# Norm weights and sub-keys of a two-layer decoder kept on chip for both chunks of a layer

## Chip, core and metric

The kernel runs on one core of one Trainium2 chip, all in float32, batch 1, 256 positions of width 1024. The metric is the device time of one execution in microseconds; the median of several executions counts.

## What is computed

Two decoder layers. Layer 0 mixes tokens with a state-space model (S5), layer 1 with dilated window attention; after each mixer stands PEER, a channel mixer that picks 16 of 16384 single-neuron experts for each of 8 heads and each token. Every sub-layer has an RMS norm with its own weight vector ahead of it, and a last norm ends the program. Cut to what matters:

```python
for i in range(2):
    h = rms_norm(x, norm_mix[i])
    x = x + (s5_mixer(h, ...) if i == 0 else dilated_attention_mixer(h, ...))
    h = rms_norm(x, norm_ffn[i])
    x = x + peer_ffn(h, peer_w_q[i], peer_sub_keys[i], peer_u[i], peer_v[i])
return rms_norm(x, norm_final)

def rms_norm(x, g):
    return x * rsqrt(mean(x * x) + 1e-6) * g

def peer_ffn(h, w_q, sub_keys, u_tab, v_tab):
    q = (h @ w_q).reshape(bsz, seq, 8, 2, 128)
    s = einsum('blhpe,hpne->blhpn', q, sub_keys)      # 16 tables of 128 keys
    ...                                               # top 16 of each half, top 16 of the sums
    act = einsum('cd,ckd->ck', hc, u_tab[ic])         # 128 experts per token
    return einsum('ck,ckd->cd', gc * gelu(act), v_tab[ic])
```

Five norm weight vectors are used: `norm_mix[0]`, `norm_ffn[0]`, `norm_mix[1]`, `norm_ffn[1]`, `norm_final`. They are rows 0 to 4 of the array `gains`.

## The kernel before

The 256 positions are two chunks of 128, one position per partition. The work of a chunk in a layer is: norm, mixer, norm, PEER scores and top-16, then the gathers of the experts. There are four gather phases (phase = 2 x layer + chunk) of 128 gathers each, 512 in all. A gather (L1233, issued by GpSimd) fetches one expert row of 8 KB (its u and its v vector) for each of the 128 partitions, 1 MB in all, into one of the eight slots of `ringmem`. Gathers come in pairs: VectorE multiplies u with the token and sums it into `dots` (L1262), ScalarE makes the gated weight (L820, L825, tile `S`), TensorE adds v (L448) and so frees the slots (semaphore `v_pe`); GpSimd issues gather s only when gather s-8 has been freed.

A chunk's gathers run beside the layer work of the next one: phase 0 beside the S5 mixer of chunk 1, phase 1 beside the attention of chunk 0, phase 2 beside the attention of chunk 1, phase 3 alone. The interleaving is written out by hand: each engine's program calls `g.at(phase, n)`, which puts the pairs up to number n ahead of the next piece of layer work. The constants at L345 to L357 (`S5_AT`, `QKV_AT`, `WO_AT` and others) set the places.

All plain loads are issued by SyncE (SP) in one fixed order, each after the waits that stand ahead of it. A weight item is 2 MB (`wt`, two buffers used in turn; item n waits for `w_used >= n-1`, the projection of item n-2). In layer 1 a chunk's items are 18 of `w_qkv`, two of `w_o`, four of `w_q`.

- One buffer `gain` (1024 floats per partition) holds the norm weight in use. `next_gain(e, n)` (L391 to L393) waits until norm number e-1 is done (`normed >= e`) and then loads row n for all partitions, 512 KB. There are nine such loads.
- The 16 key tables (`keysT`, 8 KB per partition, 1 MB) are a view into `area`, a work space that the mixers also use. So they are loaded for every phase, by `load_keys` (L395 to L397), once the mixer has left that part of `area`: behind `glu_done` in layer 0, behind `o_turned` (the transposes of the attention output, L772) in layer 1. There are four such loads. In layer 1 this load stands between the first and the second item of `w_o`, so the second item is not issued before `o_turned`.
- The users: VectorE's norm (L1287 to L1291 and L1306 to L1310) waits for `gain_in`; TensorE's score products wait for `keys_in`.

GpSimd writes the descriptors of its gathers into a part of the on-chip memory that is set aside for them, 16 KB of each partition where the program names no size.

Of the kernel before, what the change touches and what calls it, by code (L numbers as in the profile page):

```python
# [94 lines left out]
def build(nc, x, gains, lam, b_in, c_out, d_skip, w_glu, w_qkv, w_o, w_q, keys, experts, consts,  # L95
          masks, out):
    ctx = ExitStack()
    with ctx:
# [9 lines left out]
        Hrep = sb("Hrep", [P, QUAD, D])  # L108
        hT = sb("hT", [P, KT, P])
        gT = sb("gT", [P, KT, P])  # L110
        gain = sb("gain", [P, D])
        wt = sb("wt", [P, 2, KT, BLOCK])
        ringmem = sb("ringmem", [P, RING * 2 * D])
        area = sb("area", [P, A_WORDS])
# [61 lines left out]

        gflat = gT[:, :, :].rearrange("p k t -> p (k t)")
        keysT = view(area, 12288, HP, NKEYS)
        qT = view(area, 14336, 2, QHP, P)  # L180
        qs = sb("qs", [P, 512])

# [51 lines left out]
        skip_in = sem("skip_in")  # L234
        zeroed = sem("zeroed")
        wb_in = sem("wb_in")
        gain_in = sem("gain_in")
        keys_in = sem("keys_in")
        mask_in = sem("mask_in")
        w_in = [sem(f"w_in{k}") for k in range(2)]  # L240
# [119 lines left out]

        @block.sync
        def _(sp):
            sp.dma_start(small[:, 0:3, :], lam).then_inc(lam_in, 16)
            sp.dma_start(con[:, 0:C_IOTA], consts[:, 0:C_IOTA]).then_inc(ramp_in, 16)
            sp.dma_start(X[:, 0, :], x[0:P, :]).then_inc(x_in[0], 16)
            sp.dma_start(gain[:, :], gains[0:1, :].to_broadcast([P, D])).then_inc(gain_in, 16)
            sp.dma_start(WB.rearrange("p a b c -> p (a b c)"), b_in).then_inc(wb_in, 16)
            sp.dma_start(craw[:, :, :, :], c_out).then_inc(craw_in, 16)
            sp.dma_start(con[:, C_IOTA:C_ALL], consts[:, C_IOTA:C_ALL]).then_inc(con_in, 16)
            sp.dma_start(skip[:, :], d_skip).then_inc(skip_in, 16)  # L370
            sp.dma_start(X[:, 1, :], x[P:2 * P, :]).then_inc(x_in[1], 16)

            def weights(layer, c, first, last):

                for i in range(first, last):
                    n = item(layer, c, i)
                    if layer == 0:
                        src = w_glu[i] if i < WQ0 else w_q[0, i - WQ0]
                    elif i < WO:
                        src = w_qkv[i]  # L380
                    elif i < WQ1:
                        src = w_o[i - WO]
                    else:
                        src = w_q[1, i - WQ1]
                    if n == 1:
                        sp.wait_ge(glu_used, 2)
                    if n >= 2:
                        sp.wait_ge(w_used, n - 1)
                    sp.dma_start(wt[:, n % 2].rearrange("p k n -> p (k n)"), src).then_inc(w_in[n % 2], 16)

            def next_gain(e, n):  # L391
                sp.wait_ge(normed, e)
                sp.dma_start(gain[:, :], gains[n:n + 1, :].to_broadcast([P, D])).then_inc(gain_in, 16)  # L393

            def load_keys(phase, ready, count):  # L395
                sp.wait_ge(ready, count)
                sp.dma_start(keysT, keys[phase // NC]).then_inc(keys_in, 16)  # L397

            for i in range(4):
                sp.dma_start(wglu[i].rearrange("p k n -> p (k n)"), w_glu[i]).then_inc(glu_in[i], 16)  # L400
            weights(0, 0, 4, 5)
            next_gain(1, 1)
            weights(0, 0, 5, 6)
            load_keys(0, glu_done, 1)
            next_gain(2, 0)
            sp.wait_ge(glu_used, 4)
            for i in range(2):
                sp.dma_start(wq_ring[i].rearrange("p k n -> p (k n)"), w_q[0, 2 + i]).then_inc(wq_in[i], 16)
            weights(0, 1, 0, 1)
            next_gain(3, 1)  # L410
            sp.wait_ge(idx_ready, event(0, QUARTERS - 1))
            weights(0, 1, 1, 6)
            load_keys(1, glu_done, 2)
            weights(0, 1, 6, 8)
            for c in range(NC):
                next_gain(4 + 2 * c, 2)
                weights(1, c, 0, 2)
                next_gain(5 + 2 * c, 3)
                weights(1, c, 2, 8)
                sp.wait_ge(score_done, event(1 + c, QUARTERS - 1))  # L420
                n = NG * P * (c + 1)
                sp.dma_start(mask[:, 0:n], masks[:, M_AT[c]:M_AT[c] + n]).then_inc(mask_in, 16)
                weights(1, c, 8, WO + 1)
                load_keys(2 + c, o_turned, c + 1)
                weights(1, c, WO + 1, ITEMS1)
            next_gain(8, 4)
            for c in range(NC):
                sp.wait_ge(out_ready, c + 1)
                sp.dma_start(out[c * P:(c + 1) * P, :], H[:, :]).then_inc(out_done, 16)
            sp.wait_ge(out_done, 16 * NC)  # L430
# [3 lines left out]
        def _(pe):  # L434
# [93 lines left out]
            def peer_scores(gphase, layer, c, at_norm, at_wq):  # L528
# [3 lines left out]
                for i in range(QUARTERS + 1):  # L532
                    g.at(gphase, at_wq + i)
                    if i == 0:
                        pe.wait_ge(hT_ready, e + 1)
                    if i < 2:
                        spread_next(ph, (2 * i, 2 * i + 1))
                    if i < QUARTERS:
                        project_turned(item(layer, c, (WQ0, WQ1)[layer] + i), 4 + i)
                    if i == 1:  # L540
                        pe.wait_ge(keys_in, 16 * (ph + 1))
                    if i >= 1:
                        pe.wait_ge(q_copied, event(ph, i - 1))
                        for m in range(QHP):
                            hp = QHP * (i - 1) + m
                            last = pe.matmul(ps[:, 3 + i, m * P:(m + 1) * P], qT[:, (i - 1) % 2, m, :],  # L546
                                             keysT[:, hp, :], start=True, stop=True,
                                             skip_group_check=True)
                        last.then_inc(score_done, 1)
# [690 lines left out]
        def _(v):  # L1240
# [42 lines left out]
                                ALU.add).then_inc(var_ready, 1)  # L1283

            def norm_scale(c, e, done, h_free, count):
                v.wait_ge(root_ready, e + 1)
                link(v.reciprocal(stat[:, 3:4], stat[:, 2:3]))  # L1287
                v.wait_ge(gain_in, 16 * (min(e, 8) + 1))
                if count:
                    v.wait_ge(h_free, count)  # L1290
                v.scalar_tensor_tensor(out=H[:, :], in0=X[:, c, :], scalar=stat[:, 3:4],  # L1291
                                       in1=gain[:, :], op0=ALU.mult, op1=ALU.mult).then_inc(done, 1)

            def norm(gphase, start, c, e, done, h_free, count):
                norm_sum(c)
# [3 lines left out]
            def norm_halves(c, e):  # L1299
# [4 lines left out]
                                ALU.add).then_inc(var_ready, 1)  # L1304
                v.wait_ge(root_ready, e + 1)
                link(v.reciprocal(stat[:, 3:4], stat[:, 2:3]))  # L1306
                v.wait_ge(gain_in, 16 * (e + 1))
                for half in range(2):
                    cols = slice(half * 512, (half + 1) * 512)
                    v.scalar_tensor_tensor(out=H[:, cols], in0=X[:, c, cols], scalar=stat[:, 3:4],  # L1310
                                           in1=gain[:, cols], op0=ALU.mult,
                                           op1=ALU.mult).then_inc((h_half, normed)[half], 1)

            def s5_lambda():
# [447 lines left out]
```

## Time and profile before

| | us |
|---|---|
| median of 3 runs | 1752.63 (1750.5 to 1753.52) |
| span of the profiled execution | 1755.3 |

| engine | busy, us | share of the span |
|---|---|---|
| TensorE, matmul | 1285.1 | 73% |
| TensorE, weight load (beside the matmuls) | 544.9 | 31% |
| VectorE | 1120.6 | 64% |
| ScalarE | 677.5 | 39% |
| GpSimd | 616.7 | 35% |

The core's DMA engines moved 685.81 MB. The profile gives the profiled execution's span, from the first to the last instruction, and no separate time around it. In the tables of stages a DMA share of 1.0 says that all 16 DMA engines had a packet under way throughout; the rate in GB/s beside it says what they moved. "PEclk" is the granted TensorE clock as a share of full speed. In a timeline the bracket behind a row is the time in which the engine sat idle before it, with what ended it.

### The profile page before, as it was taken

Reading aid. Unit: us, or ns where it says so; the run is one execution under the profiler, and the core shown is the slowest. Engines: PE = TensorE matmul, PEld = TensorE weight load, DVE = VectorE, ACT = ScalarE, POOL = GpSimd, SP = SyncE. Lnnn points to the kernel's source line nnn. Section 1 sums busy time; section 2 is a strip of 40 time slices with the busy share of each in tenths; the row PEclk is TensorE's granted clock in tenths of the full one; section 3 lists DMA queues with packets and bytes.
Section 4 is the critical chain, followed back from the end, with each engine's and each line's share of the span. In section 5 each row is a group of like instructions: output and inputs, shape, how many; then the busy total and the mean of one; then the engine's idle time right before and its main releaser. Section 6 shows DMA issues by size and latency. Waiting matters only on the chain.

```text
span 1755.3 us, 17565 instructions
## 1 busy us (share of the span) xinstructions
PE 1285.1 (73%) x5714; PEld 544.9 (31%) x5714; DVE 1120.6 (64%) x2526; ACT 677.5 (39%) x2033; POOL 616.7 (35%) x557
## 2 busy tenths in 40 slices
PE   3876565666969968997788895899886975545454
PEld 2463111222713313333244331543451810000000
DVE  8967999863568765436347966553554567676544
ACT  7643232322243257128134333821652233233222
POOL 4213444442242243224223323332442144444442
PEclk9988877688989979998899998999997976786878
DMA  8099999999999999999999999999999899999997
GB/s 332 7 367 378 380 366 390 392 407 422 424 420 423 424 422 421 426 422 421 423 414 418 415 423 411 381 386 424 422 379 423 332 333 411 418 418 412 420 421 299
DMA packets 86636, 685.81 MB, mean 391 GB/s; under 512 B 9872, under 2 KB 10256, under 8 KB 12176
## 3 DMA queue, kind: packets, MB, share of 16 engines
q0 software_dynamic: 73728, 536.90, 74.9%
q1 hardware_dynamic: 12816, 147.79, 20.3%
q8 instruction: 45, 0.74, 0.2%
q14 instruction: 47, 0.39, 0.1%
HBM read 683.60 MB, written 1.05 MB: 390 GB/s over the span
## 4 chain that ended last, share of the span: by engine, by line
PE 34%; DMA 33%; DVE 19%; ACT 6%; issue 5%; POOL 2%; SPq 0%; POOLq 0%; ACTq 0%; DVEq 0%
DMA ringmem<-experts,lay 24%; PE ps L509 11%; PE ps L448 11%; PE ps L523 6%; DMA wt<-w_qkv 6%; DVE ringmem L1262 6%; POOL ringmem L1233 2%; DMA wt<-w_o 2%; ACT S L825 1%; ACT lay L898 1%; PE ps L727 1%; PE ps L702 1%; PE ps L461 1%; PE ps L713 1%; DMA wt<-w_glu 1%
## 5 line engine op out<-in xcount | busy, mean ns | idle before, releaser
L1233 POOL DMA_INDIRECT ringmem<-experts,lay x512 | 585.3, 1143 | 1062.4 <-PE ps L448 932.0
L448 PE MATMUL ps<-ringmem,S 128*32 128x512 f32 x2048 | 618.2, 753 | 368.3 <-ACT S L825 364.3
L1262 DVE CUSTOM_DVE_ANT_0 ringmem<-ringmem,Hrep 128x1024 f32<-128x1024 f32 x384 | 461.1, 1224 | 260.4 <-DMA ringmem<-experts,lay 257.9
L448 PEld LDWEIGHTS ps<-ringmem,S 128*32 128x32 f32 x2048 | 112.6, 126 | 761.7 <-ACT S L825 516.4
L820 ACT ACTIVATE gelus<-dots 128x2 f32<-128x2 f32 x256 | 51.5, 201 | 628.7 <-DVE dots L1262 624.0
L509 PE MATMUL ps<-wt,hT 128*128 128x512 f32 x576 | 256.2, 598 | 13.8 <-DMA wt<-w_qkv 13.8
L1262 DVE CUSTOM_DVE_ANT_0 ringmem<-ringmem,area 128x1024 f32<-128x1024 f32 x128 | 155.6, 1225 | 110.6 <-DMA ringmem<-experts,lay 110.0
L509 PEld LDWEIGHTS ps<-wt,hT 128*128 128x128 f32 x576 | 106.7, 190 | 164.1 <-issue 153.8
L816 ACT ACTIVATE S<-con,lay 128x32 f32<-128x32 f32 x512 | 134.6, 311 | 39.7 <-PE ps L448 39.1
L825 ACT ACTIVATE S<-S,gelus 128x32 f32<-128x32 f32 x512 | 136.8, 314 | 24.6 <-ACT gelus L820 1.1
L523 PEld LDWEIGHTS ps<-hT,wt 128*128 128x128 f32 x896 | 104.4, 197 | 12.1 <-issue 11.9
L523 PE MATMUL ps<-hT,wt 128*128 128x128 f32 x896 | 107.3, 282 | 0.0
L509 PE MATMUL ps<-wt,gT 128*128 128x512 f32 x128 | 63.2, 652 | 12.6 <-DMA wt<-w_o 10.5
L820 ACT ACT_TABLE_LOAD x55 | 70.6, 1283 | 1.0
L898 ACT COPY lay<-sel 32x16 f32<-32x16 f32 (+1 forms) x272 | 54.4, 200 | 18.8 <-DVE sel L1586 15.8
L1090 ACT COPY area<-ps 128x512 f32<-128x512 f32 x12 | 7.0, 586 | 135.3 <-PE ps L509 135.3
L1607 DVE TENSOR_TENSOR area<-ps,con 128x512 f32<-128x512 f32 x24 | 16.6, 690 | 65.9 <-PE ps L509 56.7
L1622 DVE CUSTOM_DVE_ANT_0 area<-ps,area 128x384 f32<-128x384 f32 (+1 forms) x32 | 24.2, 757 | 46.2 <-PE ps L702 46.2
L1510 DVE MAX8 qs<-ps 128x8 f32<-128x128 f32 x56 | 12.6, 285 | 62.0 <-PE ps L546 47.4
L1262 DVE DVE_READ_ACCUMULATOR2_ANT dots<- 128x1 f32 x512 | 42.1, 82 | 0.0
L509 PEld LDWEIGHTS ps<-wt,gT 128*128 128x128 f32 x128 | 26.1, 209 | 50.8 <-issue 34.6
L1065 ACT ACT_TABLE_LOAD x32 | 41.1, 1283 | 0.6
(234 smaller groups left out, 1237.1 us busy)
## 6 DMA issues: line engine op xcount, KB each, us to landing
wt<-w_qkv SPq DMA_DIRECT2D x36, 2048.0 KB, 11.6
wt<-w_q SPq DMA_DIRECT2D x14, 2048.0 KB, 11.3
wt<-w_glu SPq DMA_DIRECT2D x5, 2048.0 KB, 11.9
ringmem<-experts,lay POOLq DMA_INDIRECT x512, 12.5
wt<-w_o SPq DMA_DIRECT2D x4, 2048.0 KB, 14.4
ringmem<-w_glu SPq DMA_DIRECT2D x3, 2048.0 KB, 21.5
gain<-gains SPq DMA_DIRECT2D x9, 512.0 KB, 11.1
area<-keys SPq DMA_DIRECT2D x4, 1024.0 KB, 9.6
```

The costliest lines, as they stand in the source:

```text
L448: last = pe.matmul(ps[TG * t:TG * (t + 1), half, :], S[:, u % 2, i, :], ring[:, (2 * u + i) % RING, D + half * 512:D + (half + 1) * 512], ...
L461: pe.matmul(ps[:, bank, :], rep[rows_j, :], H[rows_j, half * 512:(half + 1) * 512], start=True, stop=True, skip_group_check=True).then_inc ...
L509: last = pe.matmul(ps[:, bank, :], act[:, k, :], wt[:, n % 2, k, :], start=(k == 0), stop=(k == KT - 1))
L523: last = pe.matmul(ps[:, bank, m * P:(m + 1) * P], w[:, k, m * P:(m + 1) * P], hT[:, k, :], start=(k == 0 and m == parts[0]), stop=(k == K ...
L816: last = act.activation(S[:, u % 2, i, :], own, ACT.Copy, scale=lay[:, phase % NC, 1, j - 1 + i, n:n + 1])
L820: act.activation(gelus[:, u % 2, :], dots[:, u % 2, :], ACT.Gelu_apprx_tanh).then_inc(gelu_ready, 1)
L825: last = act.activation(S[:, u % 2, i, :], S[:, u % 2, i, :], ACT.Copy, scale=gelus[:, u % 2, i:i + 1])
L898: last = act.copy(lay[TG * r:TG * (r + 1), ph % NC, :, j, n:n + width], sel[TG * j:TG * (j + 1), :, at + width * r:at + width * (r + 1)])
L1065: act.activation(SS[u % 2][:, 0:n], SS[u % 2][:, 0:n], ACT.Exp, bias=nmx[:, u:u + 1], scale=DH ** -0.5, accum_out=den[:, u:u + 1]).then_in ...
L1233: pool.indirect_dma_start(ring[:, s % RING, :], None, experts[phase // NC], bass.IndirectOffsetOnAxis(ap=rows[:, phase % NC, j, n:n + 1], ...
L1262: last = v.tensor_tensor_reduce(ring[:, i, 0:D], ring[:, i, 0:D], hrep(phase, j), 1.0, 0.0, ALU.mult, ALU.add, dots[:, b, second:second + 1])
L1622: v.tensor_tensor_reduce(SS[u % 2][:, 0:n], banks(2, 4)[:, at:at + n], mask[:, 0:n], 1.0, NEG, ALU.add, ALU.max, mx[:, u:u + 1]).then_inc( ...
```

## The change

The norm weights get two buffers, one for the norms ahead of the mixers (rows 0, 2 and 4 of `gains`) and one for the norms ahead of PEER (rows 1 and 3), and the keys get a buffer of their own outside `area`. Each weight vector is loaded once and each layer's keys once, for both chunks. That is 4 KB and 8 KB per partition more; the room for gather descriptors is cut from 16 KB to 4 KB per partition. The waits and places of the loads in SP's order change with it.

```diff
-        gain = sb("gain", [P, D])
+        gains_at = [sb("gain_mix", [P, D]), sb("gain_ffn", [P, D])]
+        keysT = sb("keysT", [P, HP, NKEYS])
...
-        keysT = view(area, 12288, HP, NKEYS)
...
-        gain_in = sem("gain_in")
+        gain_in = [sem("gain_mix_in"), sem("gain_ffn_in")]
...
+            def load_gain(n):
+                which = n % 2
+                sp.dma_start(gains_at[which][:, :],
+                             gains[n:n + 1, :].to_broadcast([P, D])).then_inc(gain_in[which], 16)
+
+            def load_keys(layer):
+                sp.dma_start(keysT[:, :, :], keys[layer]).then_inc(keys_in, 16)
...
             def next_gain(e, n):
-                sp.wait_ge(normed, e)
-                sp.dma_start(gain[:, :], gains[n:n + 1, :].to_broadcast([P, D])).then_inc(gain_in, 16)
-
-            def load_keys(phase, ready, count):
-                sp.wait_ge(ready, count)
-                sp.dma_start(keysT, keys[phase // NC]).then_inc(keys_in, 16)
+                sp.wait_ge(normed, e + 1)
+                load_gain(n)
...
             weights(0, 0, 4, 5)
-            next_gain(1, 1)
+            load_gain(1)
+            load_keys(0)
             weights(0, 0, 5, 6)
-            load_keys(0, glu_done, 1)
-            next_gain(2, 0)
             sp.wait_ge(glu_used, 4)
             for i in range(2):
                 sp.dma_start(wq_ring[i].rearrange("p k n -> p (k n)"), w_q[0, 2 + i]).then_inc(wq_in[i], 16)
             weights(0, 1, 0, 1)
-            next_gain(3, 1)
+            next_gain(norm_event(0, 1, 0), 2)
             sp.wait_ge(idx_ready, event(0, QUARTERS - 1))
-            weights(0, 1, 1, 6)
-            load_keys(1, glu_done, 2)
-            weights(0, 1, 6, 8)
+            weights(0, 1, 1, 8)
+            next_gain(norm_event(0, 1, 1), 3)
             for c in range(NC):
-                next_gain(4 + 2 * c, 2)
-                weights(1, c, 0, 2)
-                next_gain(5 + 2 * c, 3)
-                weights(1, c, 2, 8)
+                weights(1, c, 0, 8)
                 sp.wait_ge(score_done, event(1 + c, QUARTERS - 1))
+                if c == 0:
+                    load_keys(1)
                 n = NG * P * (c + 1)
                 sp.dma_start(mask[:, 0:n], masks[:, M_AT[c]:M_AT[c] + n]).then_inc(mask_in, 16)
-                weights(1, c, 8, WO + 1)
-                load_keys(2 + c, o_turned, c + 1)
-                weights(1, c, WO + 1, ITEMS1)
-            next_gain(8, 4)
+                weights(1, c, 8, ITEMS1)
+            next_gain(norm_event(1, 1, 0), 4)
...
-                        pe.wait_ge(keys_in, 16 * (ph + 1))
+                        pe.wait_ge(keys_in, 16 * (layer + 1))
...
-                v.wait_ge(gain_in, 16 * (min(e, 8) + 1))
+                v.wait_ge(gain_in[which], 16 * (min(e, 8) // 4 + 1))
...
-    nc = bacc.Bacc("TRN2", target_bir_lowering=False, num_devices=1)
+    nc = bacc.Bacc("TRN2", target_bir_lowering=False, num_devices=1, dynamic_dma_scratch_size=4096)
```

## Rows read from the trace of the kernel before

**Rows 1.** The page, what the DMA engines moved in 40 slices of 43.9 us

```profile
GB/s 332 7 367 378 380 366 390 392 407 422 424 420 423 424 422 421 426 422 421 423 414 418 415 423 411 381 386 424 422 379 423 332 333 411 418 418 412 420 421 299
```

**Rows 2.** Table of stages: start:end, length, busy by engine, PEclk, DMA share, GB/s

```profile
380.00:1095.00 715.00, 589.01 (x2282) 254.66 (x2280) 424.17 (x1043) 268.90 (x806) 223.34 (x198) 0.91 1.01 421
1200.00:1285.00 85.00, 75.99 (x348) 37.49 (x346) 41.41 (x80) 43.18 (x96) 28.66 (x26) 0.98 1.01 423
1285.00:1300.00 15.00, 12.16 (x88) 8.40 (x88) 9.87 (x19) 12.43 (x31) 7.61 (x6) 1.00 0.91 320
1307.00:1367.00 60.00, 44.74 (x139) 18.66 (x140) 22.62 (x38) 13.91 (x43) 15.70 (x15) 0.80 1.01 424
1367.00:1435.00 68.00, 58.88 (x336) 34.81 (x334) 38.85 (x116) 21.88 (x75) 20.25 (x18) 0.87 0.84 316
1435.00:1730.00 295.00, 156.13 (x472) 28.12 (x472) 186.45 (x407) 89.82 (x357) 133.28 (x118) 0.76 1.01 415
```

**Rows 3.** TensorE's waits between 380 and 1095 us: total, times, longest

```profile
PE ps L448 <- ACT S L825: 97.3, 41, 7.7
```

**Rows 4.** The page, DMA issues: issuer, count, KB each, median us to landing

```profile
gain<-gains SPq DMA_DIRECT2D x9, 512.0 KB, 11.1
area<-keys SPq DMA_DIRECT2D x4, 1024.0 KB, 9.6
```

**Rows 5.** SP's timeline: start us, us, issue; loads of gain, keys, second w_o item

```profile
110.78 0.33 SPq L393 DMA_DIRECT2D gain<-gains  x1
421.12 0.33 SPq L397 DMA_DIRECT2D area<-keys  x1
520.65 0.33 SPq L393 DMA_DIRECT2D gain<-gains  x1
848.16 0.33 SPq L397 DMA_DIRECT2D area<-keys  x1
848.53 0.43 SPq L389 DMA_DIRECT2D wt<-w_o  x1
918.46 0.79 SPq L393 DMA_DIRECT2D gain<-gains  x1
965.84 0.33 SPq L393 DMA_DIRECT2D gain<-gains  x1
1305.82 0.33 SPq L397 DMA_DIRECT2D area<-keys  x1
1306.20 0.44 SPq L389 DMA_DIRECT2D wt<-w_o  x1
```

**Rows 6.** TensorE's timeline, last w_qkv and second w_o projection of each chunk

```profile
773.40 7.13 PE L509 MATMUL ps<-wt,hT 128*128 128x512 f32 x16
864.52 10.10 PE L509 MATMUL ps<-wt,gT 128*128 128x512 f32 x16 [4.92 <-DMA wt<-w_o]
1229.39 7.10 PE L509 MATMUL ps<-wt,hT 128*128 128x512 f32 x16 [0.63 <-DMA wt<-w_qkv]
1323.44 9.34 PE L509 MATMUL ps<-wt,gT 128*128 128x512 f32 x16 [5.53 <-DMA wt<-w_o]
```

**Rows 7.** GpSimd's timeline, first gather behind the second w_o projection of chunk 1

```profile
1334.90 1.21 POOL L1233 DMA_INDIRECT ringmem<-experts,lay  x1 [14.53 <-PE ps L448]
```

**Rows 8.** TensorE's timeline, the first projection out of ringmem, no idle time before

```profile
114.96 16.66 PE L523 MATMUL ps<-hT,ringmem 128*128 128x128 f32 x128
```

**Rows 9.** The page, gather queue: packets, MB, share of 16 engines' span

```profile
q0 software_dynamic: 73728, 536.90, 74.9%
```

**Rows 10.** GpSimd's timeline, a burst of eight gathers, the first and the last

```profile
1486.36 1.38 POOL L1233 DMA_INDIRECT ringmem<-experts,lay  x1 [8.54 <-PE ps L448]
...
1496.79 1.40 POOL L1233 DMA_INDIRECT ringmem<-experts,lay  x1 [0.30 <-issue]
```

**Rows 11.** DMA issues between 150 and 330 us: gathers, median us to landing

```profile
ringmem<-experts,lay POOLq DMA_INDIRECT x64, 9.0
```

**Rows 12.** VectorE's timeline, the update of X at the end of phase 2

```profile
1427.57 1.22 DVE L1277 TENSOR_TENSOR X<-X,ps 128x1024 f32<-128x1024 f32 x1 [7.18 <-PE ps L448]
```

More of the change, by code:

```diff
@@ L365, in _ @@
             sp.dma_start(X[:, 0, :], x[0:P, :]).then_inc(x_in[0], 16)
-            sp.dma_start(gain[:, :], gains[0:1, :].to_broadcast([P, D])).then_inc(gain_in, 16)
+            load_gain(0)
             sp.dma_start(WB.rearrange("p a b c -> p (a b c)"), b_in).then_inc(wb_in, 16)
@@ L1285, in norm_scale @@
             def norm_scale(c, e, done, h_free, count):
+                which = e % 2 if e < 8 else 0
                 v.wait_ge(root_ready, e + 1)
                 link(v.reciprocal(stat[:, 3:4], stat[:, 2:3]))
-                v.wait_ge(gain_in, 16 * (min(e, 8) + 1))
+                v.wait_ge(gain_in[which], 16 * (min(e, 8) // 4 + 1))
                 if count:
@@ L1291, in norm_scale @@
                 v.scalar_tensor_tensor(out=H[:, :], in0=X[:, c, :], scalar=stat[:, 3:4],
-                                       in1=gain[:, :], op0=ALU.mult, op1=ALU.mult).then_inc(done, 1)
+                                       in1=gains_at[which][:, :], op0=ALU.mult, op1=ALU.mult).then_inc(done, 1)
             def norm(gphase, start, c, e, done, h_free, count):
@@ L1306, in norm_halves @@
                 link(v.reciprocal(stat[:, 3:4], stat[:, 2:3]))
-                v.wait_ge(gain_in, 16 * (e + 1))
+                v.wait_ge(gain_in[e % 2], 16)
                 for half in range(2):
@@ L1310, in norm_halves @@
                     v.scalar_tensor_tensor(out=H[:, cols], in0=X[:, c, cols], scalar=stat[:, 3:4],
-                                           in1=gain[:, cols], op0=ALU.mult,
+                                           in1=gains_at[e % 2][:, cols], op0=ALU.mult,
                                            op1=ALU.mult).then_inc((h_half, normed)[half], 1)
```

## Prediction, made before the changed kernel had run

> **What bounds the kernel now.** I read the page first. Its slices show over 410 GB/s for most of the span, with three exceptions: the first 110 us, in which nothing is gathered (332 and 7 GB/s), the stretch up to some 380 us (366 to 407), and single slices between 1097 and 1450 us (down to 332) [rows 1]. The table of stages says what that rate means. From 380 to 1095 us all DMA engines were busy throughout and moved 421 GB/s; the best stage moved 424, so 424 is the ceiling I use. TensorE was busy for 589 of those 715 us [rows 2]. The wait that fills most of its idle time there is for `S`, the gated weight, which hangs on a gather's landing: 97.3 us in 41 waits [rows 3]. So in this long stretch bytes are time, and TensorE is second, not far behind. From 1200 to 1285 and from 1307 to 1367 us the DMA engines are full too (423 and 424), between them and after them they are not (320 and 316) [rows 2]. The last phase has gathers alone at 415 GB/s [rows 2]. What the reader is to see: a load taken away pays where the rate stands at its ceiling, and nowhere else; an earlier load pays where an engine stands waiting for it and the DMA engines have room.
>
> **The loads that go.** Before there are nine loads of norm weights and four of keys [rows 4], after it five and two. Four loads of 0.524 MB and two of 1.049 MB go, 4.2 MB of 686. At 421 GB/s a norm weight is 1.25 us and the keys are 2.49 us. By place:
> - One norm weight load went out ahead of the first gather, in the part of the span whose slice shows 7 GB/s [rows 1]; beside it the DMA engines had little more to do than two weight items that TensorE never waited for: it ran into its first projection out of `ringmem` with no idle time [rows 8]. Worth nothing. The load at 110.78 [rows 5] is replaced by one of another row at the same place.
> - The keys at 421.12 and the norm weights at 520.65, 918.46 and 965.84 [rows 5] lie in the full stretch: 2.49 + 3 x 1.25 = 6.2 us. (Behind the last `w_q` item of layer 0 a load stays, with another row.) Bounds: 6.2 us if each byte is time, half of it, 3.1, if TensorE, busy for 82% of the stretch, takes over at every second one. I take 5.6: TensorE idles 97 us on gathers there, spread over 41 places, so a gain seldom has to go far to find one; some is lost at 918, where TensorE runs without a gap.
> - The keys at 1305.82 [rows 5] lie at the start of the full stage from 1307: 1.049 MB at 424 are 2.5 us.
>
> By the Trainium skill, DMA: Bandwidth & Descriptors, Anatomy of one DMA, a DMA costs about 2.0 us besides its bytes. If those 2.0 us were paid one after another, the six loads would be worth 12 us more than by my prices. The case's trace speaks against it: the DMA engines are at their ceiling while such a load is on its way, so its fixed part lies beside other packets.
>
> **The loads that move.** In layer 1 `load_keys` waited for `o_turned` ahead of the second `w_o` item, so that item was issued at 848.53 and 1306.20 [rows 5]. Without this wait it needs only the projection of the last `w_qkv` item, which ended at 773.40 + 7.13 = 780.5 and at 1229.39 + 7.10 = 1236.5 [rows 6]: 68 and 70 us sooner. TensorE stood 4.92 and 5.53 us for it, and the projection behind the pause took 10.10 and 9.34 us against 7.10 for its like [rows 6]. So on TensorE alone 4.9 + 3.0 = 7.9 us go in chunk 0 and 5.5 + 2.2 = 7.7 us in chunk 1. GpSimd issued nothing for 14.53 us there [rows 7]. But the bytes stay, only earlier:
> - Chunk 0 lies wholly in the full stretch. What can be won there is what the DMA engines missed, (424 - 421) / 424 of 715 us = 5 us over the entire stretch, most of it elsewhere. Bounds 0 and 7.9, and I take 0.9.
> - Chunk 1: the stages 1200 to 1285 and 1307 to 1367 are full, and the item now goes into the first. Between them 15 us ran at 320 GB/s [rows 2]: (424 - 320) / 424 x 15 = 3.7 us of room, into which the gathers pushed back by the early item can flow. Bounds for keys and item together: 2.5 (only the bytes of the keys) and 7.7 (all of TensorE's time). I take 2.5 + 2.0 = 4.5, about half of the room, because the stage behind it (1367 to 1435) hangs on TensorE, 58.9 of 68 us [rows 2].
>
> **Edits with no price.** The keys of layer 1 for chunk 0 are issued right ahead of the mask, halfway through the attention of chunk 0, instead of at 848.16 [rows 5], with the same bytes in the same full stretch; the mask behind them on SP comes some 3 us later and is first used by the attention heads, behind ten more weight items. At the start, norm weight row 1 and the keys of layer 0 go out behind the four `w_glu` items in SP's order, into the part with 7 GB/s [rows 1], so nothing that is wanted early stands behind them. Two `w_q` items go out some 5 us sooner, which nobody waits for [rows 8]. New waits: `next_gain` waits for the norm that uses the old row; each of the three stands where the items behind it need a projection that comes later than that norm. If I am wrong here, an item comes late by its 12 us once; I take 0, with 0 to 1 us either way.
>
> **The smaller room for descriptors.** The queue of the gathers shows 73728 packets [rows 9] / 512 gathers / 16 engines = 9 packets per gather and engine. Eight gathers went out in a row with 0.30 us between them [rows 10], so the old room holds at least eight; a quarter of it holds at least two. The trace doesn't show where its end lies. In the last phase a gather takes 295 / 118 = 2.5 us of the DMA engines [rows 2] and landed after 9.0 us where these were least crowded [rows 11], so 9.0 / 2.5 = 3.6 gathers must be under way to keep them full. Bounds: nothing, if four or more fit; 9.0 / 3 = 3.0 us for each gather instead of 2.5 if three fit, which is 118 x 0.5 = 59 us in the last phase alone. I take nothing: the old room never made GpSimd wait, also not in a burst of eight. By that the cost is nothing too; no row here can show it.
>
> **The sum.** 5.6 + 0.9 + 4.5 = 11.0 us. The profiled span goes from 1755.3 to 1744.3; the median of the runs is 2.7 us below that span, and 1752.6 - 11.0 = 1741.6 us. The bounds of the terms give 3.1 + 0 + 2.5 = 5.6 and 6.2 + 7.9 + 7.7 = 21.8 us, so 1747.0 and 1730.8.
>
> **Rivals.**
> 1. The bytes are hidden more than I think. For it: TensorE is busy for 82% of the full stretch, and the stages it rules (1367 to 1435) stand right behind the second gain. Then half of the first term and little of the last one arrive, 3.1 + 1.0 = 4.1 us: 1748.5. This is also the case in which the change hardly does what it says: fewer bytes, same time.
> 2. Both pauses for `w_o` pay in full, because the stoppage of GpSimd (14.5 us) is what is really given back: 6.2 + 7.9 + 7.7 = 21.8 us, 1731. Against it: the DMA engines were full through both pauses (421 and 424 GB/s). The rule on the fixed 2.0 us, named above, would come to about the same time, 1742 - 12 = 1730, and has its chance in this case; I give it a small part of it.
> 3. Slower: GpSimd runs out of descriptor room and holds gathers back although slots are free. Its place is the last phase above all, where nothing else uses the DMA engines; its price with room for three is 59 us there, about 1742 + 59 = 1801; it decides as soon as fewer than 3.6 gathers fit, and from 11 / 512 = 0.02 us per gather it would eat the gain. Against it: no waits of this kind in the trace; for it: the room is cut to a quarter, and the trace shows only that it holds two.
>
> **How the numbers follow.** Chances: my forecast 0.54, with a range of its own of 1736.5 to 1746.5; rival 1 0.22; rival 2 0.13; rival 3 0.11. About 0.2%, 3.5 us, is what a measurement of this kernel can tell from no change, so the line for faster is 1749.1. The forecast and rival 2 are faster (0.67), rival 1 lies on both sides of the line (0.11 and 0.11), of rival 3 I put 0.01 to no change and 0.10 to slower. Faster 0.78, same 0.12, slower 0.10. The range takes in rivals 1 and 2 and the bounds, 1731 to 1752, and a mild form of rival 3: 1731 to 1754; outside it lie some 0.13.
>
> **What would show each step.** The bytes should be 681.6 MB, five loads of norm weights and two of keys. The full stretch should end 6 us sooner: phase 2's first gathers and the update of X between phases 1 and 2 should come 6 us sooner. No wait of TensorE for `w_o` should be left, and the second projection should take 7.1 us in both chunks; the distance between the two projections of `w_o` in chunk 1 should fall by 7 us, and about half of that should be gone again at the end of phase 2 (the update of X that ends it at 1427.6 before [rows 12], 1416.5 after). Phase 3, from there to the end of its gathers, should keep its length; if it is longer and GpSimd waits in bursts for something other than TensorE, rival 3 holds. The prediction is wrong if the rate in the full stretch falls below 421 GB/s, or if a weight item comes late because of the new order of SP.

## The result and the profile after

| | before | after |
|---|---|---|
| median, us | 1753.52 (1750.11 to 1757.85, 9 runs) | 1743.81 (1738.55 to 1748.95, 9 runs) |
| span of the profiled execution, us | 1755.3 | 1741.3 |
| loads of norm weights and keys | 9 and 4 | 5 and 2 |

The ratio of after to before is 0.9948, with a 95% interval of 0.9932 to 0.9963: 9.1 us of 1753.5, between 6.5 and 11.9. The changed kernel's page (the slices, then the DMA queues with packets, MB and share of 16 engines' span):

```profile
GB/s 359 4 309 398 372 374 388 384 416 423 423 421 417 424 421 421 425 426 419 423 420 401 387 425 422 391 367 425 423 380 419 391 378 405 422 415 413 422 421 282
...
q0 software_dynamic: 73728, 536.90, 75.5%
q1 hardware_dynamic: 11952, 143.59, 19.7%
```

These are the rows that answer to [rows 1] and [rows 9]: the rates have kept their level, the gather queue has exactly as many packets, and the plain loads have 4.2 MB less than the 147.79 MB of before. The table of stages of after, at the same clock times as [rows 2]:

```profile
380.00:1095.00 715.00, 592.88 (x2298) 257.18 (x2298) 425.63 (x1044) 271.44 (x810) 233.57 (x200) 0.91 1.01 419
1200.00:1285.00 85.00, 71.80 (x325) 35.56 (x324) 36.98 (x70) 41.32 (x94) 25.76 (x25) 0.96 1.01 422
1285.00:1300.00 15.00, 12.17 (x84) 7.69 (x82) 10.35 (x21) 12.31 (x26) 5.72 (x4) 1.00 0.88 334
1307.00:1367.00 60.00, 51.60 (x226) 24.52 (x223) 25.51 (x42) 17.32 (x53) 20.97 (x18) 0.89 1.01 421
1367.00:1435.00 68.00, 54.38 (x293) 27.69 (x291) 49.88 (x144) 23.34 (x84) 27.64 (x22) 0.87 0.94 374
1435.00:1730.00 295.00, 156.13 (x466) 27.18 (x464) 183.06 (x391) 89.56 (x356) 121.39 (x112) 0.76 0.99 411
```

The full stretch is still full (a DMA share of 1.01), with 200 gathers issued in it instead of 198. Its rate is 419 GB/s and not 421; the prediction had named a rate below 421 as a sign of being wrong. But the kernel before, with nothing changed except the room for descriptors (the first experiment), shows 417 in the same stage, so the sign was finer than two executions agree. The room in the rate is not filled: 334 GB/s between 1285 and 1300 us, 320 before. The stage from 1367 us moves 374 instead of 316 GB/s: 347 up to 1410 us, where phase 2 ends now, and 419 behind it, where the gathers are alone. Before, phase 2 lasts until 1427 us.

TensorE's timeline of after, the four projections with `w_o`, answering to [rows 6]:

```profile
854.14 7.13 PE L508 MATMUL ps<-wt,gT 128*128 128x512 f32 x16
...
863.04 7.13 PE L508 MATMUL ps<-wt,gT 128*128 128x512 f32 x16
...
1311.94 7.13 PE L508 MATMUL ps<-wt,gT 128*128 128x512 f32 x16
...
1320.85 7.13 PE L508 MATMUL ps<-wt,gT 128*128 128x512 f32 x16
```

No bracket: the pauses of 4.92 and 5.53 us are gone, and the second projection takes 7.13 us instead of 10.10 and 9.34. But it starts at 1320.85, hardly before the 1323.44 of [rows 6], because the first one starts 3 us later than before. The pauses went, and little time went with them. In chunk 0 the pause did not even go, it moved. SP's timeline of after where the keys of layer 1 are loaded now, and TensorE's timeline at the second projection behind them:

```profile
584.07 0.43 SPq L369 DMA_DIRECT2D keysT<-keys  x1
584.54 0.43 SPq L423 DMA_DIRECT2D area<-masks  x1
...
611.22 9.01 PE L508 MATMUL ps<-wt,hT 128*128 128x512 f32 x16 [5.80 <-DMA wt<-w_qkv]
```

The kernel before has the mask alone at this place, and there the same projection starts at 609.58 behind a pause of 0.45 us and takes 7.11. Every kernel below that loads the keys here shows a pause of 5.5 to 6.1 us. This is the late weight item that the prediction named as a sign of being wrong.

VectorE's updates of X at the ends of the four phases, in after:

```profile
512.91 1.22 DVE L1276 TENSOR_TENSOR X<-X,ps 128x1024 f32<-128x1024 f32 x1
...
958.88 1.22 DVE L1276 TENSOR_TENSOR X<-X,ps 128x1024 f32<-128x1024 f32 x1 [2.15 <-PE ps L447]
...
1410.62 1.22 DVE L1276 TENSOR_TENSOR X<-X,ps 128x1024 f32<-128x1024 f32 x1 [0.24 <-PE ps L447]
...
1733.81 1.22 DVE L1276 TENSOR_TENSOR X<-X,ps 128x1024 f32<-128x1024 f32 x1 [4.59 <-PE ps L447]
```

Against 1427.57 before [rows 12], phase 2 ends 17 us sooner, and against the other updates of before,

```profile
516.17 1.22 DVE L1277 TENSOR_TENSOR X<-X,ps 128x1024 f32<-128x1024 f32 x1
...
961.37 1.22 DVE L1277 TENSOR_TENSOR X<-X,ps 128x1024 f32<-128x1024 f32 x1
...
1747.79 1.22 DVE L1277 TENSOR_TENSOR X<-X,ps 128x1024 f32<-128x1024 f32 x1 [2.88 <-PE ps L448]
```

phase 0 ends 3.3 us, phase 1 only 2.5 us and the last phase 14.0 us sooner. Read like this, phase 1, which lost two norm weight loads, gained nothing, and phase 2, which lost a norm weight load, a key table and a pause, gained 14.5 us. That was my rival reading for the experiments: the early `w_o` item of chunk 1 carries the gain.

### The profile page after: what moved, and what is told of

Read it like the earlier page. It is cut to its first block, busy times and chain, and to the rows that moved or that the text cites. A ratio compares the mean times of both kernels' runs of the same rounds, so it can differ in the third digit from the quotient of the medians.

```text
span 1741.3 us, 17559 instructions
## 1 busy us (share of the span) xinstructions
PE 1282.5 (74%) x5714; PEld 542.7 (31%) x5714; DVE 1121.0 (64%) x2526; ACT 677.7 (39%) x2033; POOL 623.3 (36%) x557
## 2 busy tenths in 40 slices
DMA packets 85772, 681.62 MB, mean 391 GB/s; under 512 B 9776, under 2 KB 10160, under 8 KB 11568
## 4 chain that ended last, share of the span: by engine, by line
PE 34%; DMA 31%; DVE 18%; ACT 7%; issue 6%; POOL 3%; ACTq 0%; DVEq 0%; POOLq 0%
DMA ringmem<-experts,lay 24%; PE ps L508 11%; PE ps L447 11%; DMA wt<-w_qkv 7%; PE ps L522 6%; DVE ringmem L1261 6%; POOL ringmem L1232 3%; ACT lay L897 2%; ACT S L824 1%; PE ps L726 1%; PE ps L460 1%; PE ps L701 1%; PE ps L712 1%; ACT L819 1%; DVE area L1622 1%
## 5 line engine op out<-in xcount | busy, mean ns | idle before, releaser
L1232 POOL DMA_INDIRECT ringmem<-experts,lay x512 | 591.8, 1156 | 1041.7 <-PE ps L447 906.6
L522 PEld LDWEIGHTS ps<-hT,wt 128*128 128x128 f32 x896 | 104.1, 196 | 11.9 <-issue 11.9
L508 PE MATMUL ps<-wt,gT 128*128 128x512 f32 x128 | 57.1, 599 | 2.1 <-DMA wt<-w_glu 2.1
L701 PE MATMUL ps<-area 64*128 64x128 f32 x288 | 41.8, 289 | 0.0
## 6 DMA issues: line engine op xcount, KB each, us to landing
wt<-w_glu SPq DMA_DIRECT2D x5, 2048.0 KB, 13.1
```

The lines of the kernel that those rows point to most:

```text
L508: last = pe.matmul(ps[:, bank, :], act[:, k, :], wt[:, n % 2, k, :], start=(k == 0), stop=(k == KT - 1))
L522: last = pe.matmul(ps[:, bank, m * P:(m + 1) * P], w[:, k, m * P:(m + 1) * P], hT[:, k, :], start=(k == 0 and m == parts[0]), stop=(k == K ...
L701: last = pe.matmul(ps[:, 2 + at // 512, at % 512:at % 512 + P], QT[rows, gr, h // 2, :], kt, start=True, stop=True, skip_group_check=True)
L1232: pool.indirect_dma_start(ring[:, s % RING, :], None, experts[phase // NC], bass.IndirectOffsetOnAxis(ap=rows[:, phase % NC, j, n:n + 1], ...
```

## The experiments

All ratios are against the kernel before, run on the same chip between the others; the changed kernel itself stands at 0.9948. It was not run again beside them, so a difference from it carries both intervals, together some 4 us to either side. 1 us is 0.00057.

**The room for descriptors alone.** The kernel before with one edit:

```diff
-    nc = bacc.Bacc("TRN2", target_bir_lowering=False, num_devices=1)
+    nc = bacc.Bacc("TRN2", target_bir_lowering=False, num_devices=1, dynamic_dma_scratch_size=4096)
```

> The kernel before with nothing changed but the room for descriptors, 4 KB instead of 16 KB per partition. My theory: the room never limits eight gathers, ratio to before 1.000 within 0.002. Rival (the smaller room holds gathers back): slower, ratio 1.005 and more, and the gain of the change as a whole would then be larger without it.

Measured: 0.9996 (0.9981 to 1.0012). The quartered room costs nothing, and the gain of the change is not a sum of a larger gain and a loss. Its profile also shows how far one execution can be read. Its row for the full stretch, and its updates of X for phases 1 and 2:

```profile
380.00:1095.00 715.00, 590.16 (x2274) 256.42 (x2272) 422.01 (x1039) 267.19 (x797) 221.69 (x196) 0.92 1.00 417
...
967.20 1.22 DVE L1277 TENSOR_TENSOR X<-X,ps 128x1024 f32<-128x1024 f32 x1 [5.00 <-PE ps L448]
...
1423.07 1.22 DVE L1277 TENSOR_TENSOR X<-X,ps 128x1024 f32<-128x1024 f32 x1 [5.98 <-PE ps L448]
```

With the same instructions as before, phase 2 takes 455.9 us here and 466.2 us in the first profile. Ten microseconds between two executions of equal work: the 14.5 us of a single pair of profiles prove little. Taken over more profiles the pattern does not go away, though. The four kernels with (nearly) all the bytes (before, this one, `bytes_back`, `both_back`) have phase 2 at 455.9 to 467.3 us, 463.1 in the mean; the four with the bytes of the change or all its extra loads at the start (after, `stall_only`, `idle_bytes`, the one with 1024 bytes) at 448.3 to 457.2 us, 452.5 in the mean. That is 10.6 of the 13.2 us by which their last updates of X differ, while only 1.57 of the 3.67 MB, 3.7 us, went out of phase 2. Why the gain shows there is open.

**The wait alone.** The changed kernel with SP's wait for the transposes put back between the `w_o` items:

```diff
-                weights(1, c, 8, ITEMS1)
+                weights(1, c, 8, WO + 1)
+                sp.wait_ge(o_turned, c + 1)
+                weights(1, c, WO + 1, ITEMS1)
```

> The changed kernel with one wait put back: SP waits for the transposes of the attention output between the two w_o items, in both chunks; no load more. By the terms of my sum the early item is worth 0.9 + 2.0 = 2.9 us, so 0.9965 of before (1747). Rival, read from the trace after (phase 2 is 14.5 us shorter, phase 1 not at all): the early item of chunk 1 carries most of the gain, so this kernel gives back 7 us or more, 0.999 of before.

Measured: 0.9949 (0.9936 to 0.9962), the changed kernel's time. Both expectations missed, mine of 0.9965 by a hair and the rival's of 0.999 clearly, and TensorE's timeline of this kernel, the `w_o` projections of both chunks, shows why:

```profile
850.62 7.16 PE L510 MATMUL ps<-wt,gT 128*128 128x512 f32 x16
...
859.55 7.13 PE L510 MATMUL ps<-wt,gT 128*128 128x512 f32 x16
...
1301.94 7.13 PE L510 MATMUL ps<-wt,gT 128*128 128x512 f32 x16
...
1311.80 7.13 PE L510 MATMUL ps<-wt,gT 128*128 128x512 f32 x16 [0.89 <-DMA wt<-w_o]
```

The wait is there and the item goes out late, and yet TensorE pauses for 0.89 us in one chunk and not at all in the other. The wait for `o_turned` does not make the pauses by itself. What stood between it and the item in the kernel before was 1 MB of keys on the same queue, and the pause at 611 us in the changed kernel, behind the same keys and no such wait, points at them too.

**The pause itself.** The changed kernel with the layer 1 keys of both chunks where the kernel before has them:

```diff
-                if c == 0:
-                    load_keys(1)
...
-                weights(1, c, 8, ITEMS1)
+                weights(1, c, 8, WO + 1)
+                sp.wait_ge(o_turned, c + 1)
+                load_keys(1)
+                weights(1, c, WO + 1, ITEMS1)
...
-                        pe.wait_ge(keys_in, 16 * (layer + 1))
+                        pe.wait_ge(keys_in, 16 * max(1, ph))
```

> The changed kernel with the layer 1 keys loaded in both chunks where the kernel before loads them: behind the wait for the transposed attention output and straight ahead of the second w_o item. That is one key table more (1.05 MB, 2.5 us in the full stretch) and should bring TensorE's pause of some 5 us back in both chunks. If the pause is hidden behind full DMA engines: 0.9962 of before. If the pause costs what I took for it, 0.9 + 2.0 us more: 0.9979. If it pays in full, as in rival 2: 1.005.

Measured: 0.9970 (0.9949 to 0.9991). TensorE's timeline of this kernel, the second `w_o` projections:

```profile
860.62 9.25 PE L509 MATMUL ps<-wt,gT 128*128 128x512 f32 x16 [5.02 <-DMA wt<-w_o]
...
1323.27 10.03 PE L509 MATMUL ps<-wt,gT 128*128 128x512 f32 x16 [5.47 <-DMA wt<-w_o]
```

Both pauses are back, with the slow projections behind them, 7.1 + 8.4 us of TensorE's time in all. The kernel is 3.9 us slower than the changed one, of which 2.5 are the price of the key table that it loads once more. So 1.4 us are left for both pauses; by the intervals of the two ratios anything from nothing to some 6 us, but not 15.6. (This kernel is rid of the pause at 611 us, which was worth 5.3 + 1.9 us of TensorE's time, so the net is 8.3 and not 15.5 us; that too is outside.) The table of stages for the pauses, in this kernel:

```profile
846.00:861.00 15.00, 9.98 (x29) 3.71 (x26) 4.16 (x8) 1.50 (x8) 4.22 (x4) 0.90 1.01 425
1308.00:1323.00 15.00, 9.81 (x30) 3.33 (x24) 3.17 (x6) 2.70 (x12) 3.87 (x5) 0.98 1.01 427
```

While TensorE waits, the DMA engines run at 425 and 427 GB/s. The pause takes nothing that can be seen from the resource that sets the time.

**The bytes, all.** The changed kernel, with three norm weights and two key tables loaded again, and the early `w_o` item kept:

```diff
-            weights(0, 1, 1, 8)
+            weights(0, 1, 1, 6)
+            sp.wait_ge(glu_done, 2)
+            load_keys(0)
+            weights(0, 1, 6, 8)
...
-                weights(1, c, 0, 8)
+                if c:
+                    sp.wait_ge(normed, norm_event(1, 0, 1) + 1)
+                    load_gain(2)
+                weights(1, c, 0, 2)
+                sp.wait_ge(normed, norm_event(1, c, 0) + 1)
+                sp.wait_ge(gain_in[1], 16 * (2 + c))
+                load_gain(3)
+                weights(1, c, 2, 8)
...
-                weights(1, c, 8, ITEMS1)
+                weights(1, c, 8, WQ1 + 1)
+                if c:
+                    load_keys(1)
+                weights(1, c, WQ1 + 1, ITEMS1)
```

> The changed kernel with the early w_o item, but three norm weights and two key tables loaded again (3.7 MB) at about the places where the kernel before loads them, without a wait that holds up the items behind. By my sum the bytes are worth 5.6 + 2.5 = 8.1 us, so 0.9994 of before. Rival (the early item carries the gain, bytes are hidden behind TensorE): under 3 us back, 0.9965 or less.

Measured: 0.9993 (0.9972 to 1.0014), 7.9 us above the changed kernel (3.3 to 12.5), against 8.1 expected and under 3 of the rival. The loads account for nearly the whole change. That 7.9 meets 8.1 so closely is luck, with such an interval.

**Both.** The two edits together, the wait of `stall_only` and the loads of `bytes_back`.

> The changed kernel with both put back, the wait and the 3.7 MB. Both theories: the time of the kernel before, ratio 1.000 within 0.002, if buffers of their own and the start add nothing. If it stays at 0.997 or less, a third part carries some of the gain: the start, or the place of the layer 1 keys.

Measured: 1.0003 (0.9987 to 1.0020), the time of the kernel before, and 9.6 us above the changed kernel (5.6 to 13.6). Of the pauses only the wait is in it: TensorE's second `w_o` projections of both chunks in this kernel

```profile
864.06 7.13 PE L523 MATMUL ps<-wt,gT 128*128 128x512 f32 x16
...
1322.35 7.13 PE L523 MATMUL ps<-wt,gT 128*128 128x512 f32 x16 [0.41 <-DMA wt<-w_o]
```

start behind no pause and one of 0.41 us, and the pause at 611 us is there as in the changed kernel (5.99 us, with a projection of 8.50 us). So the kernel before, with 15.6 us at its two `w_o` pauses against 6.9 + 0.4 us here, is at most 2.3 us slower, by the lower end of the interval. This is the sharpest bound on what the pauses are worth. Buffers of their own, the early start of the first keys and the moved keys of layer 1 add nothing that can be seen.

**The bytes in two parts.** The norm weights alone, which is the second hunk above, and the keys alone, the first and the third.

> The changed kernel with three norm weight loads put back in layer 1 (1.57 MB, the places of the kernel before), nothing else. If bytes in the full stretch are time, 3.7 us back: 0.9969 of before. If TensorE hides them (rival 1), under 1 us: 0.9953 or less. If each load also pays a fixed time of 2 us, 9.7 us: 1.000 and more.

> The changed kernel with two key table loads put back (2.10 MB, one beside the layer 0 scores of chunk 1, one behind the w_o items of chunk 1), with no wait ahead of them that holds up others. Bytes are time: 5.0 us back, 0.9976 of before. Hidden: 0.9955 or less. Together with the three norm weights the sum must come to the 7.9 us between the changed kernel and the one with all these bytes.

Measured: 0.9960 (0.9942 to 0.9978) and 0.9984 (0.9962 to 1.0005), that is 2.1 us for 1.57 MB and 6.3 us for 2.10 MB above the changed kernel, 8.4 together. The split into single loads is finer than the intervals of 4 to 5 us to either side allow; what they exclude is the 9.7 us for the norm weights by a fixed time for each load.

**The same loads at the start.** The changed kernel with two key tables and three norm weights loaded again one after another, right at the start:

```diff
             load_keys(0)
+            for k in (1, 2):
+                sp.wait_ge(keys_in, 16 * k)
+                load_keys(0)
+            for k in (1, 2, 3):
+                sp.wait_ge(gain_in[1], 16 * k)
+                load_gain(1)
```

> The changed kernel with as many loads more (two key tables, three norm weights, 3.67 MB), but all at the start, one after another before the first gather, where a slice shows 4 GB/s. If place decides and not the amount: no difference from the changed kernel, 0.9948 within 0.0015. If every load costs wherever it lies: 0.9993, like the kernel that has them in the full stretch.

Measured: 0.9932 (0.9911 to 0.9953), not slower than the changed kernel (2.8 us below it, within 4.6 to either side). SP's timeline shows where they went, all before the first gather:

```profile
8.46 39.29 SPq L369 DMA_DIRECT2D keysT<-keys  x3
47.80 9.71 SPq L365 DMA_DIRECT2D gain_ffn<-gains  x3
```

The same 3.7 MB are worth 7.9 us in the full stretch and nothing here.

**More bytes, in two places.** The changed kernel with the layer 1 keys loaded five times more (5.24 MB), beside the second half of the `w_qkv` items of chunk 0 or, with `c == 1` in the first line, of chunk 1:

```diff
+                if c == 0:
+                    for r in range(5):
+                        weights(1, c, 8 + 2 * r, 10 + 2 * r)
+                        sp.wait_ge(keys_in, 16 * (2 + r))
+                        load_keys(1)
+                    weights(1, c, 18, ITEMS1)
+                else:
+                    weights(1, c, 8, ITEMS1)
```

> The changed kernel with the layer 1 keys loaded five times more (5.24 MB), one behind every second w_qkv item of the second half of chunk 0, in the full stretch (423 GB/s between 600 and 770 us in the changed kernel). Bytes are time: 12.4 us more than the changed kernel, 1.0019 of before. If TensorE, 83% busy there, hides half of it: 0.9983. If a load costs 2 us besides its bytes: 1.0076.

> The same five loads beside the second half of chunk 1's projections and first attention heads, where TensorE was busy for 114 of 125 us (1090 to 1215) and the DMA engines moved 393 GB/s. Room by (424 - 393) / 424 x 125 = 9 us, so if place decides, 12.4 - 9 = 3.4 us: 0.9967 of before. If the amount alone decides: 1.0019 like its twin.

Measured: 1.0029 (1.0011 to 1.0047) and 1.0023 (1.0007 to 1.0038). In chunk 0 that is 14.2 us above the changed kernel (10 to 18.4), 12.4 expected; half of it hidden (6.2) and a fixed time for each load (22.4) are both outside. In chunk 1 it is 13.1 us where I expected 3.4, and the reason is in SP's timeline of that kernel, three of its rows:

```profile
1056.14 0.43 SPq L369 DMA_DIRECT2D keysT<-keys  x1
...
1167.32 0.94 SPq L369 DMA_DIRECT2D keysT<-keys  x1
...
1228.43 0.43 SPq L369 DMA_DIRECT2D keysT<-keys  x1
```

Between the weight item of 1066 and that of 1167 us none is issued, so none of the loads went out there, and those are the attention heads, where the room in the rate was (374 GB/s from 1090 to 1167 us in the changed kernel, and 424 from 1167 to 1215; my 393 was the mean of the two). All five loads lie in full stages: 423 GB/s from 1039 to 1090, 420 from 1167 to 1215, where three of them went out, and 423 from 1215 to 1285 in this kernel. So this run says nothing on a load in a stage in which the DMA engines have room beside a busy TensorE; that stays open.

**How small the room may be.** The changed kernel with 1024 and with 512 bytes per partition in place of 4096.

 By the bound of 3.6 gathers in flight this costs nothing: the changed kernel's 0.9948 within 0.002. If the end of the room at each pass costs GpSimd a stop, it is slower by some tenths of a per cent, with waits of GpSimd that TensorE didn't cause.

> The changed kernel with 512 bytes per partition, by the same estimate 32 descriptors and three gathers. By my bound (three in flight give 9.0 / 3 = 3.0 us for each gather instead of 2.5) the last phase alone becomes 59 us longer, so 1.03 of before or more, and GpSimd waits between issues for something that is not TensorE. If the room is not what holds gathers back at all, 0.9948.

Measured: 0.9955 (0.9939 to 0.9970) and 1.0628 (1.0587 to 1.0670). From the kernel with 512 bytes, two of GpSimd's waits and a stage of the last phase:

```profile
POOL ringmem L1232 <- issue: 837.3, 436, 8.1
...
POOL ringmem L1232 <- PE ps L447: 159.4, 72, 7.9
...
1500.00:1800.00 300.00, 155.55 (x398) 25.78 (x400) 161.97 (x355) 79.84 (x313) 149.98 (x100) 0.63 0.95 350
```

GpSimd's idle time has changed hands: 837.3 us that nothing in the profile releases ("issue") and 159.4 us for TensorE, where the changed kernel has 92.1 and 906.6 us. 100 gathers in 300 us are 3.0 us each, at 350 GB/s. The last phase alone takes 379.6 us, 56.4 more than in the changed kernel, where 59 were expected; the other 63 us of this kernel's loss lie in the phases ahead of it, which I had not priced.

How many gathers the 512 bytes hold can be read off directly. GpSimd's timeline, and VectorE's, where a bracket of DMA says when the gather that it waited for landed:

```profile
1599.25 1.57 POOL L1232 DMA_INDIRECT ringmem<-experts,lay  x1 [2.86 <-issue]
...
1608.89 1.68 POOL L1232 DMA_INDIRECT ringmem<-experts,lay  x1 [3.78 <-issue]
1611.35 1.57 POOL L1232 DMA_INDIRECT ringmem<-experts,lay  x1 [0.78 <-issue]
...
1608.53 1.22 DVE L1261 CUSTOM_DVE_ANT_0 ringmem<-ringmem,Hrep 128x1024 f32<-128x1024 f32 x1 [1.18 <-DMA ringmem<-experts,lay]
...
1610.88 1.23 DVE L1261 CUSTOM_DVE_ANT_0 ringmem<-ringmem,Hrep 128x1024 f32<-128x1024 f32 x1 [1.12 <-DMA ringmem<-experts,lay]
```

The gather of 1599.25 lands at 1608.53 and the next but two is issued at 1608.89; again at 1610.88 and 1611.35. With VectorE's n-th row matched to the n-th gather, 103 gathers of the last phase can be dated in this way: at 101 of the landings exactly two later gathers were out, and at 100 the next issue followed within 0.6 us. So the room holds three. In the changed kernel and in the one with 1024 bytes four or five later ones are out at most landings of the last phase, and never more than six.

## Why the prediction was right

The forecast was 1741.6 us from a base of 1752.6, a gain of 11.0 us; measured are 9.1 us, within its own range of 1736.5 to 1746.5. Step by step:

- *A load pays where the rate stands at its ceiling, and nowhere else.* Held. The loads of the full stages (5.6 + 2.5 = 8.1 us) measured 7.9 us when put back (3.3 to 12.5; with the wait, 9.6, 5.6 to 13.6), and nothing when put at the start. Five tables more in chunk 0 cost 2.7 us for each MB, the rate of 421 GB/s makes it 2.4.
- *The fixed 2.0 us of a DMA lie beside other packets.* Held: with them three norm weights would have cost 9.7 us; measured are 2.1 (at most some 6), and five key tables cost 14.2 us and not 22.4. The section of the Trainium skill that the prediction named (DMA: Bandwidth & Descriptors, Anatomy of one DMA) fits its 2.0 us to DMAs that GpSimd issues, and these loads are SP's. No run here measures one load by itself; among others the fixed part isn't paid one after another.
- *The early second item of `w_o`, 0.9 + 2.0 us.* The step with a wrong cause. I read the pause off SP's order and blamed the wait for `o_turned`. With the wait alone put back, there is no time lost and hardly a pause; with the 1 MB of keys between the wait and the item the pause is back, and the same keys moved the pause of chunk 0 to 611 us in the changed kernel. As for its worth, all of it is 1.4 us by one pair of kernels and 1.2 us by the rest of the sum (9.1 - 7.9), with intervals that include nothing and my 2.9. The prediction's excess of 1.9 us over the measured gain is of the size of this term, and no larger than the measurement's own interval (6.5 to 11.9 us), so that the sum came this close is in part luck. That the 15.6 us of TensorE in rival 2 do not pay is shown: the pauses were back in full and the time wasn't, and the kernel before is at most 2.3 us slower than `both_back`, which has 8 us less of them.
- *The room for descriptors, nothing.* Held down to a quarter of the new size. The bound of 3.6 gathers in flight held as well: no loss that can be seen at 1024 bytes, a loss at 512, and there the 3.0 us per gather that I had worked out for three gathers. One reading of mine was wrong: the burst of eight in [rows 10] lasts 10.4 us, and the first two of its gathers had landed (at 1493.21 and 1496.15) before the eighth went out at 1496.79. It shows that the old room holds six, and a quarter of that is one, so the trace left rival 3 more ground than I gave it.
- *Edits with no price.* The mechanism failed, the price held. I wrote that nothing comes late by the keys' new place ahead of the mask; a `w_qkv` item did, and TensorE stands 5.80 us for it at 611 us. The DMA engines are full there (423 GB/s from 600 to 770 us), and with wait and bytes put back, this pause included, what is left of the change is at 1.0003, within 2 to 3 us to either side.
- *What the profile would show.* 681.62 MB and the second `w_o` projections at 7.13 us without a pause came as written. The ends of the phases did not: phase 1 was to end 6 us sooner and ended 2.5 us sooner, the two `w_o` projections of chunk 1 moved together by 5.6 us and not 7, phase 2 ended at 1410.6 and not at 1416.5, and the last phase took 323.2 instead of 320.2 us. Two executions of the same instructions differ there by ten microseconds, so these signs were finer than one profile can carry, and so was the rate of 421 GB/s (419 came, with 417 in a kernel that moves all the bytes).

Of the rivals, the hidden bytes (1748.5, 4.1 us) fall with the 9.6 us of `both_back` (5.6 at the least) and the 14.2 us of the five tables, which the 7.9 us alone would not do; the full pauses (1731) fall with `pause_back` and `both_back`, and the lack of room is true of a room eight times smaller than the one chosen.

One thing stays open: why phase 2 gained 10.6 us in the mean for 3.7 us of bytes. From the second `w_o` projection of chunk 1 to the end of phase 2 it takes 97.1 to 104.1 us, at a granted clock of 0.81 to 0.86 of full speed, in the five kernels before, `room4k_before`, `bytes_back`, `both_back` and `keys_back`, which all load a key table at 1305 us or later; in the seven others with 4096 or 1024 bytes and no such load it takes 89.7 to 97.9 us at 0.84 to 0.92. So TensorE's clock may carry a part of the gain there. But `pause_back`, which loads that table at the same place as before, takes 91.6 us at 0.91, so the load alone does not bring the longer times. The times of the whole kernels (8.1 expected, 7.9 and 9.6 measured) neither need such a part nor exclude a few microseconds of it.

## What to carry to other kernels

Where the DMA engines stand at their ceiling, price a load by its bytes at that ceiling first; in this kernel neither a pause of TensorE nor the load's own latency added anything that could be seen while other packets kept the engines full. On-chip memory that saves a second load of the same data is worth that price: here 12 KB of each partition bought some 8 us (3 to 13 by the intervals). The room for gather descriptors can be such memory as long as it still holds the gathers that have to be under way, which is landing time over the time between two gathers. And ask what a load stands ahead of on its queue: a wait that vanishes at one place can turn up at the next.

## What the runs showed of the hardware

- With the room for descriptors cut to 512 bytes per partition, nothing fails; GpSimd holds the next gather back, and the profile books it as idle time that nothing released. 4096 and 1024 bytes show no loss, and of such time 92.1 and 90.7 us against 86.7 before (837.3 with 512).
- A 2 MB item alone behind a wait arrived in time or nearly so (pauses of 0 to 0.89 us), with gathers beside it; the same item behind 1 MB on the same queue made TensorE wait 5.02 and 5.47 us, twice the 2.5 us that this 1 MB takes at 424 GB/s. The wait scatters: in two executions of the kernel before it was 4.92 and 2.04 us in chunk 0, 5.53 and 5.63 in chunk 1.
- With room for three gathers they land after 8.65 us (median of the 103 dated ones in the last phase); with four or five others out beside them, as in the changed kernel mostly, after 12.54 us (95 dated ones).
- A phase of equal work differs by 10 us between executions whose whole spans (1755.3 and 1750.9 us) differ by 4.4.
